# Two of the eight channel tiles of a 31-tap depthwise convolution computed on TensorE, four taps by 32 channels per stationary tile, on four column groups

## The reference, cut to what matters

```python
def conformer_conv(a, conv_w, conv_b, norm_g, norm_b, w_o):
    gl = a[..., :CONV_WIDTH_2] * jax.nn.sigmoid(a[..., CONV_WIDTH_2:])      # 256 x 1024
    y = lax.conv_general_dilated(gl, conv_w[:, None, :], window_strides=(1,),
                                 padding=[(CONV_PAD, CONV_PAD)],             # 31 taps, pad 15
                                 dimension_numbers=('NWC', 'WIO', 'NWC'),
                                 feature_group_count=CONV_WIDTH_2) + conv_b  # one filter a channel
    y = jax.nn.silu(layer_norm(y, norm_g, norm_b))
    return y @ w_o
```

## Time and profile before

| | us |
|---|---|
| median of 3 runs | 2186.89 (2186.88 to 2187.64) |
| the profiled execution | 2187.78 |
| its span, first to last instruction | 2185.8 |
| TensorE busy (matmul) | 2086.1, 95% |
| VectorE busy | 1566.2, 72% |
| ScalarE busy | 1129.9, 52% |
| GpSimd busy | 97.2, 4% |

### The profile page before, as it was taken

The page is one execution under the profiler, slowest core; times in us unless marked ns, Lnnn a source line. Parts: engine busy times, 40 slices in busy tenths (PEclk is TensorE's granted clock), DMA queues, the critical chain, the costliest instruction groups (busy, mean ns, idle before and its releaser), DMA issues.

```text
span 2185.8 us, 31557 instructions
## 1 busy us (share of the span) xinstructions
PE 2086.1 (95%) x12389; PEld 1785.9 (82%) x12389; DVE 1566.2 (72%) x2436; ACT 1129.9 (52%) x1571; POOL 97.2 (4%) x184
## 2 busy tenths in 40 slices
PE   7998989999999999999999999899999999997997
PEld 6776879888877788988887788698978878877996
DVE  5566466577679978655687898765677789976565
ACT  5554444445575446544557544454545674454543
POOL 3100001110000000000000000000000000000000
PEclk9999999999999999999999999999999999999999
DMA  7745467766666645677654444656555444454663
GB/s 253 225 148 188 146 223 249 235 190 203 216 211 193 195 151 168 222 220 227 189 179 130 145 135 142 214 157 191 170 174 184 131 143 126 154 164 145 189 187 106
DMA packets 206371, 394.36 MB, mean 180 GB/s; under 512 B 16471, under 2 KB 19219, under 8 KB 206224
## 3 DMA queue, kind: packets, MB, share of 16 engines
q1 hardware_dynamic: 198624, 381.74, 54.9%
q0 software_dynamic: 7600, 10.61, 1.7%
HBM read 390.98 MB, written 1.30 MB: 179 GB/s over the span
## 4 chain that ended last, share of the span: by engine, by line
PE 83%; DVE 8%; ACT 5%; issue 2%; DMA 2%; DVEq 0%; ACTq 0%; SPq 0%
PE gps L1142 15%; PE gps L1144 14%; PE gps L1143 14%; PE gps L1149 9%; PE gps L1150 9%; PE gps L1151 9%; PE aps L981 2%; PE aps L1104 2%; DVE wlo L1958 2%; PE aps L937 2%; DVE Yc L1801 2%; ACT whi L1464 1%; PE aps L1080 1%; PE aps L1111 1%; PE aps L1067 1%
## 5 line engine op out<-in xcount | busy, mean ns | idle before, releaser
L1958 DVE TENSOR_TENSOR wlo<-raw,whi 128x1024 fp32r<-128x1024 f32 (+1 forms) x648 | 763.3, 1186 | 449.6 <-ACT whi L1464 447.2
L1464 ACT ACTIVATE whi<-raw 128x1024 fp32r<-128x1024 f32 (+1 forms) x648 | 662.6, 1028 | 662.7 <-PE gps L1144 420.2
L1142 PE MATMUL gps<-whi,ohi 128*128 128x512 f32 x1624 | 656.2, 404 | 9.5 <-DVE olo L1829 5.0
L1144 PE MATMUL gps<-whi,olo 128*128 128x512 f32 x1624 | 634.8, 391 | 0.0
L1143 PE MATMUL gps<-wlo,ohi 128*128 128x512 f32 x1624 | 634.4, 391 | 0.0
L1149 PE MATMUL gps<-ohi,whi 128*128 128x256 f32 x1760 | 508.4, 289 | 1.0 <-issue 1.0
L1150 PE MATMUL gps<-olo,whi 128*128 128x256 f32 x1760 | 499.8, 284 | 0.0
L1151 PE MATMUL gps<-ohi,wlo 128*128 128x256 f32 x1760 | 499.5, 284 | 0.0
L1142 PEld LDWEIGHTS gps<-whi,ohi 128*128 128x128 f32 x1624 | 305.8, 188 | 87.2 <-issue 21.0
L1144 PEld LDWEIGHTS gps<-whi,olo 128*128 128x128 f32 x1624 | 305.5, 188 | 65.3
L1149 PEld LDWEIGHTS gps<-ohi,whi 128*128 128x128 f32 x1760 | 339.0, 193 | 20.0 <-issue 19.1
(11 more groups left out here) (284 smaller groups left out, 1544.9 us busy)
## 6 DMA issues: line engine op xcount, KB each, us to landing
raw<-w_in SPq DMA_DIRECT2D x232, 512.0 KB, 3.9
raw<-w_ff SPq DMA_DIRECT2D x192, 512.0 KB, 3.8
raw<-ada_w SPq DMA_DIRECT2D x96, 512.0 KB, 4.4
raw<-w_attn_o SPq DMA_DIRECT2D x24, 512.0 KB, 3.4
raw<-w_gmlp_o SPq DMA_DIRECT2D x24, 512.0 KB, 3.4
raw<-w_conv_o SPq DMA_DIRECT2D x24, 512.0 KB, 3.7
raw<-w_out SPq DMA_DIRECT2D x24, 512.0 KB, 4.7
raw<-w_gate SPq DMA_DIRECT2D x20, 512.0 KB, 4.1
```

Source lines behind the costliest of these rows:

```text
L1142: mm(om, ah, whi[:, q, i, :], start=first, stop=False)
L1144: t = mm(om, al, whi[:, q, i, :], start=False, stop=last)
L1464: A_(part(whi, jb, q), raw_part(jb, q), ACT.Copy).then_inc(hi_done[q], 1)
L1958: tt(part(wlo, jb, q), raw_part(jb, q), f32(part(whi, jb, q)), ALU.subtract).then_inc(lo_done[q], 1)
```

## The change

Channel tiles 3 and 7 (the last of each half) leave VectorE and ScalarE; tiles 0 to 2 and 4 to 6 have all their 31 taps on VectorE now (tap 0 on ScalarE). `diag`, `diag_mm` and `diag_add` go.

Tiles 3 and 7 are computed by a step `ck`, one for each half. A stationary tile has 128 rows, 4 taps by 32 channels, and 32 columns, the channels; 8 such tiles cover 32 taps (the last one zero), and four groups g of 32 channels go to the four groups of 32 output partitions. The moving operand `packed(half)` holds `GLP` four times, shifted by 0, 8, 16 and 24 positions, so that a block b = 0 to 7 reads it at offset b. These copies (`rep`) are 16 DMAs for each half from GpSimd, from SBUF to SBUF, 32 partitions of 263 elements each. The stationary tiles are laid out on the host (`conv_diag`) and loaded by SyncE as one 512 KB item through the `raw` ring. ScalarE evacuates with the factor 0.5 and the bias. The number of taps that each job gets on VectorE (`CONV_AT`) is new, and branch3 is a host now.

```diff
+PW = S + 7
-                  "gate3", "branch2"]
-    CONV_AT = {"x": [0, 0, 1, 2, 1, 3, 3, 0, 3, 4, 5, 5, 6, 6, 6, 6], "c": [2, 2, 0, 2, 1, 3, 3, 0, 2, 4, 4, 6, 6, 5, 6, 5]}
-
-    CONV_PE_AT = [(name, q) for name in ("gate2", "gate3", "branch2") for q in range(3)]
+                  "gate3", "branch2", "branch3"]
+    CONV_AT = {"x": [1, 1, 1, 2, 2, 4, 4, 1, 4, 6, 5, 6, 5, 5, 5, 4, 4], "c": [2, 2, 1, 2, 2, 3, 4, 1, 3, 4, 5, 6, 6, 5, 5, 5, 4]}
...
-        pe_taps = range(TAPS2 - len(CONV_PE_AT), TAPS2)
-        ops = [(half, tap) for half in range(2) for tap in range(1, TAPS2) if half == 0 or tap not in pe_taps]
-        slots = [(J[name], q) for name in ("gate2", "gate3", "branch2", "branch3") for q in range(NQ)]
-        for tap, (name, q) in zip(pe_taps, CONV_PE_AT):
-            jb, at_q = slots[slots.index((J[name], q)) + 2]
-            dg = put(J[name], q, "diag", l=l, tap=tap)
-            put(jb, at_q, "diag_mm", of=dg, job=gg1, first=tap == pe_taps[0], last=tap == pe_taps[-1])
+        ops = [(half, tap) for half in range(2) for tap in range(1, TAPS2)]
+        put(ba[0], 2, "rep", glu=(gg0, gg1), of=at[-1])
+        cks = [put(gates[2], 1, "ck", l=l, half=0), put(bg[0], 1, "ck", l=l, half=1)]
         for name, n in zip(CONV_NAMES, CONV_AT[s]):
             for q in range(NQ):
                 for half, tap in ops[n * q // NQ:n * (q + 1) // NQ]:
                     put(J[name], q, "conv", half=half, l=l, of=cv0[half], taps=[tap])
             ops = ops[n:]
-        put(bg[1], 0, "diag_add", of=dg)
-        lm = put(gates[4], 0, "ln_mu", l=l, rb_free=("t_pe", t_g, 4, 4))
+        lm = put(gates[4], 0, "ln_mu", l=l, of=cks[1], rb_free=("t_pe", t_g, 4, 4))
...
+            elif k == "ck":
+                use(p, (0,), ("ck_cp", p, 1, 1))
...
-            stream += [(p, None) for p in host.aux[host_q] if p.kind == "ada"]
+            stream += [(p, None) for p in host.aux[host_q] if p.kind in ("ada", "ck")]
...
+                if q is None and x.kind == "ck":
+                    sp.dma_start(raw[:, at % RING].rearrange("p a b -> p (a b)"), A["conv_diag"][x.l, x.half]).then_inc(loaded[at % RING], 16)
...
+            def copies(p):
+
+                for half in range(2):
+                    wait(pool, ev("gl_o", p.glu[half]), ev("at_s", p.of, 2, 2) if half == 0 else ev("at_pv", p.of))
+                    for g in range(4):
+                        for t in range(4):
+                            pool.dma_start(packed(half)[32 * t:32 * t + 32, g, :], GLP[32 * g:32 * g + 32, 4 * half + 3, 8 * t:8 * t + PW]
+                                           ).then_inc(sem[f"rep_in{half}"], 16)
...
-            def diag_mm(p):
+            def ck(p):
 
                 free(p)
-                wait(pe, ev("gl_o", p.job), ev("dg_ready", p.of))
-                for i in range(4):
-                    t = mm(aps[:, i // 2, (i % 2) * S:(i % 2 + 1) * S], Pb[:, p.of.n % 2, i * P:(i + 1) * P],
-                           GLP[:, 4 + i, p.of.tap:p.of.tap + S], start=p.first and i % 2 == 0, stop=p.last,
-                           skip_group_check=True)
-                t.then_inc(sem["dg_used"], 1)
+                pe.wait_ge(sem[f"rep_in{p.half}"], 16 * 16 * (p.n // 2 + 1))
+                pe.wait_ge(loaded[p.at % RING], 16 * (p.at // RING + 1))
+                w = raw[:, p.at % RING].rearrange("p a b -> p (a b)").rearrange("p (b g c) -> p b g c", b=8, g=4)
+                for b in range(8):
+                    for g in range(4):
+                        t = mm(aps[32 * g:32 * g + 32, 0, p.half * S:(p.half + 1) * S], w[:, b, g, :], packed(p.half)[:, g, b:b + S],
+                               start=b == 0, stop=b == 7)
+                t.then_inc(sem["ck_used"], 1)
...
-                wait(pe, ev("cv_done", None, 0, p.conv_after), ("dg_add", None, 0, p.n + 1))
+                wait(pe, ev("cv_done", None, 0, p.conv_after), ev("ck_cp", p.of))
...
-                for k in range(4 * p.half, 4 * p.half + 4):
+                for k in range(4 * p.half, 4 * p.half + 3):
...
+            def ck(p):
+                act.wait_ge(sem["ck_used"], p.n + 1)
+                k = 4 * p.half + 3
+                A_(Yc[:, k * S:(k + 1) * S], aps[:, 0, p.half * S:(p.half + 1) * S], ACT.Identity, scale=0.5,
+                   bias=C2[:, 44 * p.l + 32 + k:44 * p.l + 33 + k]).then_inc(sem["ck_cp"], 1)
...
-                    for i in range(4):
+                    for i in range(3):
```

More of the change, by code:

```diff
@@ L66, in __init__ @@
         self.po = args.get("po")
+        self.glu = args.get("glu")
         self.solo, self.early = args.get("solo"), args.get("early")
@@ L568, in make_plan @@
             elif k == "conv":
[L569 to L577, removed]
+                conv_ops += 3 * len(p.taps)
+            elif k == "ck":
+                use(p, (0,), ("ck_cp", p, 1, 1))
             elif k == "ln_mu":
@@ L621 @@
 ge_sq ge_z ge_t ge_out gl_a gl_th gl_o gn_ss gn_done sp_pe sp_done
-ln_mean ln_d ln_sq ln_vs ln_n ln_th ln_r ln_hi ln_lo ga_th br_out cv_first cv_done dg_ready dg_used dg_add ws_in ws_pe ws_cp
+ln_mean ln_d ln_sq ln_vs ln_n ln_th ln_r ln_hi ln_lo ga_th br_out cv_first cv_done rep_in0 rep_in1 ck_used ck_cp ws_in ws_pe ws_cp
 r2_relu r2_sq r2_hi r2_lo ac_cp ac_add y_add y_sq y_cp po_x out_st
@@ L656, in build @@
         kvb = sb("kvb", [P, 4, 2 * S])
-        Pb, PTb = sb("Pb", [P, 2, 2 * S]), sb("PTb", [P, 4 * S])
+        PP = sb("PP", [P, 8 * S])
+        Pb, PTb = PP[:, 0:4 * S].rearrange("p (m k) -> p m k", m=2), PP[:, 4 * S:8 * S]
         AB = sb("AB", [P, 4 * S])
-        GLP = sb("GLP", [P, KT, S + 2 * PAD2])
+        GLP = sb("GLP", [P, KT, S + 2 * PAD2 + 2])
         Yc = sb("Yc", [P, 8 * S])
@@ L724, in ada_weight, with packed @@
             return A[f"ada{p.l}"][2 * p.j * P:2 * (p.j + 1) * P, p.c * NW:(p.c + 1) * NW].rearrange("(k p) n -> p k n", p=P)
+        def packed(half):
+            return (qT[:, :] if half == 0 else PP[:, :])[:, 0:4 * PW].rearrange("p (g x) -> p g x", g=4)
         def part(t, jb, q):
@@ L760, in _ @@
                     if prev_q is None:
-                        sp.wait_ge(sem["ad_used"], prev.n + 1)
+                        sp.wait_ge(sem["ad_used" if prev.kind == "ada" else "ck_used"], prev.n + 1)
                     else:
                         sp.wait_ge(lo_done[prev_q], prev.i + 1)
-                if q is None:
+                if q is None and x.kind == "ck":
+                    sp.dma_start(raw[:, at % RING].rearrange("p a b -> p (a b)"), A["conv_diag"][x.l, x.half]).then_inc(loaded[at % RING], 16)
+                elif q is None:
                     sp.dma_start(raw[:, at % RING], ada_weight(x)).then_inc(loaded[at % RING], 16)
@@ L885, in ada @@
                                            stage[32 * h + v:32 * h + v + 65:64, :]).then_inc(sem["ad_st"], 16)
-            stages = dict(wsT=ws_load, ada=ada, toep=toep, ba=ba, ctx_load=ctx_load, modfin=modfin, modT=mod_t, gb=gb, tab=tab)
+            def copies(p):
[5 more added lines that the diff above has]
+                                           ).then_inc(sem[f"rep_in{half}"], 16)
+            stages = dict(wsT=ws_load, rep=copies, ada=ada, toep=toep, ba=ba, ctx_load=ctx_load, modfin=modfin, modT=mod_t, gb=gb, tab=tab)
             for jb in jobs:
@@ L1125, in _ @@
                           modT=mod_t, tq=tq, tk=tk, at=at, atT=atT, atV=atV, spatial=spatial, wsT=ws_t,
-                          diag_mm=diag_mm, ln_mu=ln_mu, ln_var=ln_var)
+                          ck=ck, ln_mu=ln_mu, ln_var=ln_var)
             def unit(jb, q):
@@ L1324, in conv0 @@
                 t.then_inc(sem["cv_first"], 1)
[L1326 to L1330, removed]
-                for i in range(4):
-                    t = A_(Pb[:, p.n % 2, i * P:(i + 1) * P], ident[:], ACT.Copy,
-                           scale=CW[:, p.l, p.tap * KT + 4 + i:p.tap * KT + 5 + i])
-                t.then_inc(sem["dg_ready"], 1)
+            def ck(p):
[3 more added lines that the diff above has]
+                   bias=C2[:, 44 * p.l + 32 + k:44 * p.l + 33 + k]).then_inc(sem["ck_cp"], 1)
             def ln_mu(p):
@@ L1362, in _ @@
                           maT=maT, maV=maV, wsT=wsT_, tq=tq, tk=tk, atE=atE, atS=atS, atT=atT, atH=atH, gv_sq=gv_sq,
-                          conv0=conv0, diag=diag, ln_mu=ln_mu, ln_out=ln_out)
+                          conv0=conv0, ck=ck, ln_mu=ln_mu, ln_out=ln_out)
             def late(p):
-                return p.kind in ("conv0", "diag") or p.kind == "ada" and not p.early
+                return p.kind == "conv0" or p.kind == "ada" and not p.early
             def cp(jb, g):
@@ L1799, in conv @@
                         else:
-                            dve.wait_ge(sem["cv_done"], conv_ops[0] - 3)
+                            dve.wait_ge(sem["cv_done"], conv_ops[0] - 2)
                         stt(y, x, CW[:, p.l, tap * KT + k:tap * KT + k + 1], y, ALU.mult, ALU.add).then_inc(sem["cv_done"], 1)
                         conv_ops[0] += 1
```

(15 more changed lines are left out.)

## The result

Over twenty runs of each kernel, taken together, the median went from 2188.06 to 2191.1 us (2188.27 to 2193.67); the ratio is 1.0013 with a 95% interval of 1.0007 to 1.0019. The changed kernel is 3 us slower (1.5 to 4.2 by that interval): a difference that twenty runs can tell, and under the 0.2% at which the forecast drew its line. The profiled execution has a span of 2189.0 us, 3.2 more than before.

The account below looks back on a forecast made before the run. TensorE was taken as the bound, with VectorE nearly full beside it. -47.0 + 25.3 + 20.4 + 6.0 - 1.5 + 1.0 = +4.2 us gave a forecast of 2191.1 us, range 2176 to 2203.

Parts of the forecast that it names:

- Removed and added on TensorE: On TensorE 27 `diag_mm` steps go, 47.0 us; six `ck` calls of 4.2 us come, 25.3 us.
- The new wait: TensorE stops before `ln_mu` for VectorE's last tap after branch3: 6.6, 6.6 and 7.2 us, 20.4 in all.
- The clock: Behind each new pause TensorE runs at a lowered clock: 2.0 us each, 6.0 in all.
- Loads in c: In the c mixer's gate3 and branch2 the same loads fall in less time: 1 us added, bounds 0 and 4.
- The layer norm's later wait: At the norm VectorE is found idle, not 0.7 us late: 0.5 us a mixer given back, -1.5.
- Copies and attention: GpSimd's copies hidden before `ck` (cover 25 us, need 21), no cost; attention 0, bounds -6 and +4.
- A: Rival: tap at 5.2 us, no clock fall, shorter attention waits, 2175 us; halfway, without the attention part, 2181; chance 0.22.
- C: Rival: c mixer bound by DMA, later VectorE delays heads, pauses of 8 us; 2203 us, chance 0.16.
- D: Rival: column groups don't run side by side in `ck`, 14 us a call, +58, 2250 us; chance 0.04.
- B: Rival: no pause before the norm, the whole 22 us come through, 2165 us; chance 0.08.

Follow-up runs that it names:

- e1_taps_ahead: Changed kernel with the four taps hosted by branch3 moved to gate2, gate3 and branch2; 2164.84 us, ratio 0.9894 to the kernel before.
- e2_add_late: Kernel before the change with `diag_add` moved from quarter 0 to quarter 3 of branch3; 2208.38 us, ratio 1.0093.
- e3_fill_pause: Changed kernel with 13 dead fp32 matmuls on TensorE before its wait for the last tap; 2183.51 us, ratio 0.9982 to the kernel before.
- e6_groups_outer: e1_taps_ahead with the two loops of `ck` swapped, all eight blocks of one column group before the next; 2210.25 us.

## Why the prediction was right

The forecast was 2191.1 us, and 2191.1 was measured. The sum had +4.2 and the runs gave +3.0; the rest of the agreement is that the kernel before had its median at 2186.9 when the forecast was made and at 2188.1 in the runs that decide. The mechanism is the one forecast, the new pause and the clock behind it; that the size came out this close is in part luck, since four terms were off and nearly made up for each other. Point by point, from the trace of the changed kernel:

- **Removed and added on TensorE.** `diag_mm` was put at 47.0 in all. A call of `ck` was put at 4.2: it takes 3.60 for its records and 0.2 more until matmuls follow at their pitch. The next block follows after 0.43 us (3.60 - 0.57 over seven), not 0.48: the 0.24 from one set of records to the next in rows 5 was taken for the steady pitch, and it is the first one of a call. That is 0.4 a call, 2.4 us in all, by which this term was too large; the lower bound, 3.5, had used the right pitch. From the transposes in branch1 to the end of branch3 TensorE gained 8.1 us in each x mixer, forecast 7.3, and 6.8 in c: 23.1 in all, against 47.0 - 25.3 = 21.7 in the sum.
- **The new wait.** Forecast 6.6, 6.6 and 7.2; measured 6.51, 6.51 and 6.93. The parts fit too: VectorE came 1.6 us late (forecast 1.7), and the order evacuation, split, tap is the one read from the code. e1_taps_ahead takes it away and e2_add_late makes it in the other kernel.
- **The clock.** Forecast 2.0 a pause; the first sum was longer by 1.7 and 2.1 us in the x mixers and by 2.5 in c, 6.3 in all, and e3_fill_pause got back 6.2 us in the three mixers where 6.0 had been set.
- **Loads in c.** 1.0 us was set for waits of TensorE for loads. In gate2 to branch3 none over 0.15 us came, though the DMA engines were at 0.92 and 306 GB/s from 731 to 742 us; but TensorE lost 1.6 us there in another way. Both kernels wait 2.33 us for an `ada` copy; before, the granted clock stays at 1.00 behind it, and in the changed kernel it falls to 0.50 for a while, behind the wait that ends at 744.27:

```profile
745.30:748.70 3.40, 3.40 (x10) 2.63 (x9) 2.28 (x6) 0.00 (x0) 1.51 (x3) 0.50 0.71 205
```

  Why it falls here and not before, no run shows. The 1.6 us are already in the 6.8 above.

- **The layer norm's later wait.** I gave back 1.5 us; it is 4.9 against 5.0, so nothing came. VectorE was idle when the sum ended, as said, but the chain of the norm did not end earlier against TensorE. This is a term that failed, 1.5 us too low, and it made up for most of the excess in `ck`.
- **Copies and attention.** GpSimd's 96 copies took 0.5 us each to issue and 2.7 to 2.8 to land (median, the two lines below). No `ck` waited for one: each call starts 0.2 to 0.3 us after the matmul before it, so the cover held. Attention was put at zero and was not zero. In the x mixers TensorE has new waits of 1.18 us before one head and 0.74 behind `tq`, partly offset by shorter ones; it is 2.1 us behind the kernel before at the worst place of layer 0 and 1.2 at the end of its heads, 0.9 at the end of those of layer 1 (0.5 of it from a clock that was low before the mixer began) and 0.3 ahead in c: some 1.8 us, inside the bounds around the zero that I took.

```profile
qT<-GLP POOLq DMA_DIRECT2D x48, 32.9 KB, 2.7
PP<-GLP POOLq DMA_DIRECT2D x48, 32.9 KB, 2.8
```

Of the rivals, A's halfway case (2181) would have needed a pause of 5.2 us and a clock that stays up (with the clock up alone, in e3_fill_pause, it is 2183.5), C waits for loads in c that did not come, and D was out with the first call, 3.60 us. B, no pause, has its number confirmed by e1_taps_ahead: 2164.8 measured, 2165 worked out. Together the parts read from the two traces give -23.1 + 20.0 + 6.3 + 1.8 = +5.0, not +4.2. The traces themselves differ by 5.4 us in the three mixers and by 1.4 between 1381 and 1574 us, behind a pause that both kernels have and where nothing was changed; the changed kernel's trace was 3.7 us ahead when its first mixer began, which leaves the 3.2 us between the spans. Such differences are as large as the one forecast: the profiled executions differ by up to 5.7 us before 490 us, where all these kernels are the same (a transpose that all share starts between 485.2 and 490.9 us), and the medians of the kernel before moved from 2186.9 to 2188.7 from one set of runs to the next.

## What to carry to other kernels

When work is spread over the slots of a schedule, ask of the last slot before each consumer what stands ahead of it in its engine's order: a small step behind an evacuation that waits for the consumer's own engine costs that engine a full stop, here 20 us of pauses and 6 of clock against 23 gained, and moving four taps a mixer to earlier jobs gave all of it back. Where two engines are both full, relief of one can be lost on the other (31 us taken from TensorE bought 9 before VectorE was relieved, 18.2 bought 17.6 after); test which one binds by leaving work out of one. With small stationary tiles, go round the column groups from matmul to matmul (3.6 us) rather than finish one group first (11.4 us).

## What the runs showed of the hardware

- Dead matmuls in a wait of 6.5 us kept the granted clock at 1.00 (0.73 and 0.67 without them) and made the kernel 7.6 us faster, 6.2 of it in the three places.
- Four fp32 matmuls of 256 columns with 128 x 32 stationary tiles in four column groups take 0.43 us together (3.60 for 32, in six calls); one with a 128 x 128 tile takes 0.41 in the norm's sum (3.26 / 8) and 0.44 in `diag_mm` (1.74 / 4). With the loops swapped (e6_groups_outer) 32 took 11.44 us instead of 14: by the starts, TensorE began on the next group while two matmuls of the last were still to come.
- A pause of 4.93 us was enough each time for TensorE to run below its full clock afterwards: the sums behind it took 4.92, 5.03 and 6.13 us instead of 3.26, for the same pause, so the price varies by 1.2 us from place to place. A pause of 2.33 us in c was followed by a granted clock of 0.50 in the changed kernel and by a full clock in the kernel before.
